# First norm of a two-layer decoder trunk: its factors moved into weight splits and copies, x loaded in halves, TensorE busy from the start

## The chip, the cores and the metric

The kernel runs on one core of one Trainium2 chip. The metric is the device time of one execution in microseconds (us). Three runs of the kernel before gave 1243.56 to 1244.70 us, with a median of 1244.01 us.

## What is computed

The program is a decoder trunk of two layers for 512 tokens of 1024 channels in float32. Only its opening matters here: the first norm and the input projection of the first layer.

```python
def rms_norm(x, g):
    y = x * lax.rsqrt(jnp.mean(x * x, axis=-1, keepdims=True) + NORM_EPS)
    return y * g

h = rms_norm(x, mix_norm_g[0])                     # (512, 1024)
a_q, a_k, a_v, b_q, b_k, b_v = split(h @ ab_w_in)  # 3072 columns
a_q, a_k = apply_rope(a_q), apply_rope(a_k)        # then differential attention, 4 heads
```

Each row of `h` has one factor of its own (the inverse root of its mean square), and each channel has one gain.

## The kernel before

Tokens lie in four tiles of 128 (`t` 0 to 3). A matmul works on single-precision values in three passes: weights and activations are each split into a high part (`w_hi`, `hT_hi`) and what is left of them (`w_lo`, `hT_lo`), and the products hi·hi, hi·lo and lo·hi are added up in one bank of the matmul's accumulator memory `ps`. ScalarE makes the high parts, VectorE or GpSimd the low ones.

The opening runs as follows. For each token tile ScalarE squares `x` and adds up (`square`), VectorE and ScalarE make the inverse root (`tile_variance`, `root`, `rsqrt`), VectorE multiplies `x` by root and gain in one instruction over 1024 channels (`scale_x`, to `xn`). TensorE turns the tile in eight 128x128 pieces (`turn_xn`); ScalarE copies them out in two instructions of 512 columns (`turn_tile`, high part), VectorE takes the low part (`tile_lows`). TensorE then multiplies by the first 384 columns of the projection (`group_0(t, half)`: 12 matmuls of 384 columns for each half of the channels). These 384 columns are what one group of two heads needs. The weights come in tiles of 1536 columns (`w_raw`, two slots), one for each half of the channels.

After group 0 two pieces of the next group's projection are made (`part_product(1, u, ...)`). They need the weights' third tile, split by ScalarE (`split_hi(0, 2)`) and VectorE (`split_lo(2, 0)`). Rotary positions of group 0 are applied on GpSimd for tiles 0 and 1 and on VectorE for tiles 2 and 3 (`rope(2)`, `rope(3)`); TensorE turns the results (`turn_qk`, 12 transposes), ScalarE and VectorE split them (`head_highs`, `head_lows`), and attention begins with `scores("A", 0, 0)` (line L1577), followed by the next part of the projection (L1525) in a loop over four groups.

The order on each engine is written by hand; engines wait for each other by semaphores. Loads are issued by SyncE in the order of its code. The kernel is a list of such hand-made stages; what follows the opening is attention, an MLP, the second layer and a last norm.

## Time and profile before

| | |
|---|---|
| median of three runs | 1244.01 us |
| the profiled execution's own time | 1244.71 us |
| its span (first to last instruction) | 1242.9 us |
| TensorE busy | 1215.6 us, 98% |
| VectorE, ScalarE, GpSimd busy | 512.1, 483.5, 567.8 us |

The span is what the trace covers; 1.8 us of the execution lie around it. Times below are counted from the start of the span. A busy TensorE is one with a matmul in flight, at either clock.

### The profile page before, as it was taken

Reading aid. Unit: us, or ns where it says so; the run is one execution under the profiler, and the core shown is the slowest. Engines: PE = TensorE matmul, PEld = TensorE weight load, DVE = VectorE, ACT = ScalarE, POOL = GpSimd, SP = SyncE. Lnnn points to the kernel's source line nnn. Section 1 sums busy time; section 2 is a strip of 40 time slices with the busy share of each in tenths; the row PEclk is TensorE's granted clock in tenths of the full one; section 3 lists DMA queues with packets and bytes.
Section 4 is the critical chain, followed back from the end, with each engine's and each line's share of the span. In section 5 each row is a group of like instructions: output and inputs, shape, how many; then the busy total and the mean of one; then the engine's idle time right before and its main releaser. Section 6 shows DMA issues by size and latency. Waiting matters only on the chain.

```text
span 1242.9 us, 16982 instructions
## 1 busy us (share of the span) xinstructions
PE 1215.6 (98%) x6252; PEld 1042.5 (84%) x6256; DVE 512.1 (41%) x907; ACT 483.5 (39%) x698; POOL 567.8 (46%) x501
## 2 busy tenths in 40 slices
PE   6999999999999999999999999999999999999997
PEld 6999999888888888888889879878888888888886
DVE  6777767745121211332342265634412221232325
ACT  4454544435232222433333365443523232333334
POOL 1444455334444444566655331611444444456662
PEclk9999999999999999999999999999999999999999
DMA  7212211212222222222213210300322222222221
GB/s 265 102 67 71 99 69 68 69 68 85 102 101 101 101 94 91 85 102 101 102 68 119 102 69 35 136 35 34 119 101 73 98 100 101 101 85 91 95 102 68
DMA packets 17037, 114.23 MB, mean 92 GB/s; under 512 B 1888, under 2 KB 2016, under 8 KB 4320
## 3 DMA queue, kind: packets, MB, share of 16 engines
q1 hardware_dynamic: 16416, 111.51, 24.8%
q10 hardware_dynamic: 576, 2.10, 0.6%
q8 instruction: 31, 0.51, 0.2%
q14 instruction: 14, 0.11, 0.0%
HBM read 111.50 MB, written 2.10 MB: 91 GB/s over the span
## 4 chain that ended last, share of the span: by engine, by line
PE 88%; POOL 4%; DVE 3%; ACT 1%; issue 1%; DMA 1%; POOLq 0%; SPq 0%; DVEq 0%; ACTq 0%
PE ps L1448 38%; PE ps L1738 16%; PE ps L1525 6%; PE ps L1391 6%; PE ps L1493 4%; PE ps L1420 3%; PE ps L1851 2%; PE ps L1438 2%; PE ps L1566 2%; PE ps L1831 2%; POOL tmp L327 1%; PE ps L1774 1%; POOL qk L333 1%; PE ps L1552 1%; PE ps L1348 1%
## 5 line engine op out<-in xcount | busy, mean ns | idle before, releaser
L303 POOL TENSOR_TENSOR w_lo<-w_raw,w_hi 128x512 fp32r<-128x512 f32 (+1 forms) x326 | 457.7, 1434 | 530.2 <-ACT w_hi L382 471.3
L382 ACT ACTIVATE w_hi<-w_raw 128x2048 fp32r<-128x2048 f32 (+1 forms) x95 | 175.3, 1845 | 309.6 <-PE ps L1448 155.2
L1448 PE MATMUL ps<-hT_hi,w_hi 128*128 128x512 f32 x688 | 267.7, 389 | 0.0
L1448 PE MATMUL ps<-hT_hi,w_lo 128*128 128x512 f32 x688 | 267.7, 389 | 0.0
L1448 PE MATMUL ps<-hT_lo,w_hi 128*128 128x512 f32 x688 | 267.6, 389 | 0.0
L1448 PEld LDWEIGHTS ps<-hT_lo,w_hi 128*128 128x128 f32 x688 | 129.1, 188 | 27.0
L1448 PEld LDWEIGHTS ps<-hT_hi,w_lo 128*128 128x128 f32 x688 | 129.1, 188 | 26.7
L1448 PEld LDWEIGHTS ps<-hT_hi,w_hi 128*128 128x128 f32 x688 | 129.1, 188 | 26.6
L1115 DVE TENSOR_TENSOR hT_lo<-region,hT_hi 128x2048 fp32r<-128x2048 f32 (+1 forms) x22 | 58.9, 2686 | 144.0 <-ACT hT_hi L640 144.0
L1085 DVE SCALAR_TENSOR_TENSOR qk<-ps,vec,qk 128x511 f32<-128x511 f32 x44 | 33.0, 750 | 200.1 <-ACT qk L614 200.1
L614 ACT ACTIVATE qk<-ps,vec 128x512 f32<-128x512 f32 x44 | 34.3, 780 | 175.5 <-PE ps L1448 166.3
L1738 PE MATMUL ps<-w_hi,hT_hi 128*128 128x512 f32 x256 | 99.6, 389 | 0.0
L1738 PE MATMUL ps<-w_lo,hT_hi 128*128 128x512 f32 x256 | 99.6, 389 | 0.0
L1738 PE MATMUL ps<-w_hi,hT_lo 128*128 128x512 f32 x256 | 99.6, 389 | 0.0
L1095 DVE TENSOR_TENSOR region<-ps,qk 128x512 f32 (+1 forms) x44 | 30.4, 691 | 155.4 <-PE ps L1448 155.4
L327 POOL TENSOR_TENSOR tmp<-region,cst 128x256 f32<-128x256 f32 x30 | 30.3, 1010 | 123.1 <-DVE region L926 98.4
L1525 PE MATMUL ps<-w_hi,hT_hi 128*128 128x384 f32 x224 | 80.5, 360 | 0.2 <-ACT region L498 0.2
L1525 PE MATMUL ps<-w_hi,hT_lo 128*128 128x384 f32 x224 | 75.2, 336 | 0.0
L1525 PE MATMUL ps<-w_lo,hT_hi 128*128 128x384 f32 x224 | 74.1, 336 | 0.0
L1738 PEld LDWEIGHTS ps<-w_lo,hT_hi 128*128 128x128 f32 x256 | 48.0, 188 | 10.0
L1738 PEld LDWEIGHTS ps<-w_hi,hT_hi 128*128 128x128 f32 x256 | 48.0, 188 | 10.0
L1738 PEld LDWEIGHTS ps<-w_hi,hT_lo 128*128 128x128 f32 x256 | 48.0, 188 | 9.9
(235 smaller groups left out, 2102.0 us busy)
## 6 DMA issues: line engine op xcount, KB each, us to landing
w_raw<-weights SPq DMA_DIRECT2D x99, 1024.0 KB, 4.8
x<-x_in SPq DMA_DIRECT2D x4, 512.0 KB, 8.8
gain<-gains ACTq DMA_DIRECT2D x4, 512.0 KB, 3.5
out<-region SPq DMA_DIRECT2D x4, 512.0 KB, 2.6
w_raw<-weights SPq DMA_DIRECT2D x2, 768.0 KB, 8.0
cst<-consts SPq DMA_DIRECT2D x1, 640.0 KB, 11.9
gain<-gains SPq DMA_DIRECT2D x1, 512.0 KB, 4.2
region<-masks SPq DMA_DIRECT2D x1, 384.0 KB, 12.2
```

The source lines that it names most:

```text
L303: ins = pool.tensor_tensor(w_lo[:, slot, cols], w_raw[:, slot, cols], w_hi[:, slot, cols].bitcast(f32), ALU.subtract)
L327: own.mark(pool.tensor_tensor(t1, src, cos, ALU.mult))
L382: sc.activation(w_hi[:, slot, 0:used], w_raw[:, slot, 0:used], ACT.Copy).then_inc(w_hi_ready, 1)
L614: sc.activation(qk[:, s, :], ps[:, s, :], ACT.Identity, scale=vec[:, ds(8 * i + (col + 2), 1)], bias=vec[:, ds(8 * i + (col + 3), 1)]).the ...
L1085: own.link(ve.scalar_tensor_tensor(qk[:, s, 1:SEQ], ps[:, s, 0:SEQ - 1], vec[:, ds(8 * i + (col + 1), 1)], qk[:, s, 1:SEQ], ALU.mult, ALU. ...
L1115: ve.tensor_tensor(hT_lo[:, places, :], act[:, ds(kt, count), :], hT_hi[:, places, :].bitcast(f32), ALU.subtract).then_inc(act_lo[l], count)
L1391: ins = pe.matmul(ps[:, bank, :], h[:, k0 + k, t * 128:(t + 1) * 128], w[:, slot, k * 512:(k + 1) * 512], start=first and (k, m) == produc ...
L1420: ins = pe.matmul(ps[:, s, 256 * half:256 * half + 256], w[:, slot, k * 256 + 128 * s:k * 256 + 128 * s + 128], h[:, k, 256 * half:256 * h ...
L1448: ins = pe.matmul(bank, w[:, slot, k * pitch + 128 * s:k * pitch + 128 * s + 128], h[:, k:k + 1, :], start=k == 0 and n == 0, stop=k == KT ...
L1493: ins = pe.matmul(ps[:, bank or 4 + f % 2, :], h_[:, place + k, t * 128:(t + 1) * 128], w_[:, (n0 + c) % 2, k * 512:(k + 1) * 512], start= ...
L1525: ins = pe.matmul(ps[:, bank, 0:384], h_[:, 4 * half + k, t * 128:(t + 1) * 128], w_[:, half, k * 384:(k + 1) * 384], start=first and k == ...
L1738: ins = pe.matmul(ps[:, 4 * c + t, :], a[:, t * 128:(t + 1) * 128], w[:, slot, u * 512:(u + 1) * 512], start=first and u == units[0] and n ...
```

## The change

- `x` is turned as it is, without root or gain. The gain of a channel is one number for each partition once the channels lie on partitions, and is put in where the high and low parts are made: `gained_high` on ScalarE and `gained_low` on VectorE, each four instructions of 128 columns with the gain as a per-partition operand, in place of one or two of 512 columns without one. The gains lie in `cst`, and the 512 KB load of the first gain row is gone.
- The inverse root of each token goes into the copies out of `ps` for all eight groups of the first projection (`copy_whole`, `add_part`, `copy_low`), as a per-partition operand `rstd_in`. One chain computes it for all four tiles.
- `x` is loaded in halves of 512 channels, tile 0's first half on ScalarE's queue; the identity and the first half of the first weight tile are issued first.
- TensorE multiplies eight times with a tile of ones that nothing reads (`warm`).
- All four tiles go through the first half of the channels, then all four through the second. VectorE now makes the third weight tile's low part ahead of both `rope` calls, and TensorE makes all passes of the two parts ahead of `turn_qk`.
- `copy_low(1, 0, 4)` stands ahead of `head_highs(0)`; `ident_bf`, `mask_bf` and `sub_gain` are made behind the ropes.

```diff
+        def load_x(eng, t0, t1, c, loaded):
+            src = x_in[0, t0 * 128:t1 * 128, c:c + 512].rearrange("(t p) n -> p t n", p=128)
+            eng.dma_start(x[:, t0:t1, c:c + 512], src).then_inc(loaded, 16)
...
-        FIRST_BANK = (6, 2, 4, 6)
+        FIRST_BANK = (6, 7, 2, 3)
+        FIRST_TURN = (0, 1, 4, 5)
...
-            load_x(sp, 0)
-            sp.dma_start(gain[:, :], gains[:, 0, :]).then_inc(gain_loaded, 16)
             sp.dma_start(cst[:, 0:C_CMUL], consts[:, 0:C_CMUL]).then_inc(ident_loaded, 16)
-            load(0, 0, IN_COLS)
-            load_x(sp, 1)
+            sp.dma_start(w_raw[:, 0, 0:768], weights[0, :, 0:768]).then_inc(first_loaded, 16)
+            sp.dma_start(w_raw[:, 0, 768:IN_COLS], weights[0, :, 768:IN_COLS]).then_inc(w_loaded[0], 16)
+            load_x(sp, 1, 2, 0, front_loaded[1])
+            load_x(sp, 2, 4, 0, front_loaded[2])
             load(1, 1, IN_COLS)
-            for t in range(2, NT):
-                load_x(sp, t)
+            load_x(sp, 0, 4, 512, back_loaded)
             sp.dma_start(cst[:, C_CMUL:], consts[:, C_CMUL:]).then_inc(cst_loaded, 16)
...
                 sc.wait_ge(mm_done, 8 * g + (u + 1))
-                sc.activation(y[:, u, ds(384 * g, 384)], ps[:, bank, 0:384], ACT.Copy).then_inc(part_low, 1)
+                sc.activation(y[:, u, ds(384 * g, 384)], ps[:, bank, 0:384], ACT.Copy, scale=rstd_in[:, u:u + 1])\
+                  .then_inc(part_low, 1)
...
+            load_x(sc, 0, 1, 0, front_loaded[0])
             sc.preload_act_table_set("sqrt_and_others")
-            square(0, 0)
-            root(0, 1)
+            def gained_high(half, t):
+                sc.wait_ge(turned, 4 * half + t + 1)
+                for j in range(4):
+                    k = 4 * half + j
+                    ins = sc.activation(hT_hi[:, k, t * 128:(t + 1) * 128], ps[:, FIRST_TURN[t], 128 * j:128 * j + 128],
+                                        ACT.Copy, scale=cst[:, C_GAIN + k:C_GAIN + k + 1])
+                ins.then_inc(turn_hi, 1)
+            def square_in(t):
+                scratch = stage_mem[:, :] if t else tmp[:, :, :].rearrange("p a n -> p (a n)")
+                sc.activation(scratch, x[:, t, :], ACT.Square, accum_out=ss[:, t:t + 1]).then_inc(ss_ready, 1)
...
+            gained_high(0, 0)
             sc.wait_ge(w_loaded[0], 16)
-            sc.activation(w_hi[:, 0, 0:768], w_raw[:, 0, 0:768], ACT.Copy).then_inc(w_hi_ready, 1)
-            turn_tile(0)
-            square(0, 1)
+            sc.activation(w_hi[:, 0, 768:IN_COLS], w_raw[:, 0, 768:IN_COLS], ACT.Copy).then_inc(w_hi_ready, 1)
+            gained_high(0, 1)
+            gained_high(0, 2)
             split_hi(1, 1, IN_COLS)
-            root(1, 2)
...
+            gained_high(0, 3)
+            sc.wait_ge(front_loaded[0], 16)
+            sc.wait_ge(back_loaded, 16)
+            square_in(0)
+            gained_high(1, 0)
+            sc.wait_ge(front_loaded[1], 16)
+            square_in(1)
+            gained_high(1, 1)
+            gained_high(1, 2)
+            root(0, 4)
+            gained_high(1, 3)
             turns[0] += 1
...
-            for n in range(2):
...
+            sc.wait_ge(mm_done, 1)
+            split_hi(0, 2, IN_COLS)
             sc.wait_ge(lam_dots, 1)
             sc.activation(lam_s[:, 2:4], lam_s[:, 0:2], ACT.Exp).then_inc(lam_exps, 1)
+            sc.wait_ge(mm_done, 8)
+            split_hi(1, 2, IN_COLS)
+            sc.wait_ge(scale_ready, 1)
+            copy_low(1, 0, 4)
+            head_highs(0)
...
                 ve.wait_ge(mm_done, (2, 4, 6, 8)[t])
-                ve.tensor_copy(y[:, t, 0:384], ps[:, FIRST_BANK[t], 0:384]).then_inc(part_sum, 1)
+                ve.tensor_scalar(y[:, t, 0:384], ps[:, FIRST_BANK[t], 0:384], rstd_in[:, t:t + 1], None, ALU.mult)\
+                  .then_inc(part_sum, 1)
...
                 ve.wait_ge(part_low, 4 * (g - 1) + (u - 3))
                 dst = y[:, u - 4, ds(384 * g, 384)]
-                ve.tensor_tensor(dst, dst, ps[:, 4 + u % 2, 0:384], ALU.add).then_inc(part_sum, 1)
+                ve.scalar_tensor_tensor(dst, ps[:, 4 + u % 2, 0:384], rstd_in[:, u - 4:u - 3], dst, ALU.mult, ALU.add)\
...
+            def gained_low(half, t):
+                ve.wait_ge(turn_hi, 4 * half + t + 1)
+                for j in range(4):
+                    k = 4 * half + j
+                    hi = hT_hi[:, k, t * 128:(t + 1) * 128]
+                    ins = ve.scalar_tensor_tensor(hT_lo[:, k, t * 128:(t + 1) * 128],
+                                                  ps[:, FIRST_TURN[t], 128 * j:128 * j + 128],
+                                                  cst[:, C_GAIN + k:C_GAIN + k + 1], hi.bitcast(f32),
+                                                  ALU.mult, ALU.subtract)
+                ins.then_inc(turn_lo, 1)
...
+            def first_part_low(cols, made):
+                ve.tensor_tensor(w_lo[:, 0, cols], w_raw[:, 0, cols], w_hi[:, 0, cols].bitcast(f32),
+                                 ALU.subtract).then_inc(made, 1)
+            ve.wait_ge(first_loaded, 16)
+            ve.tensor_copy(w_hi[:, 0, 0:768], w_raw[:, 0, 0:768]).then_inc(first_high, 1)
             ve.wait_ge(first_high, 1)
-            split_lo(0, 0, IN_COLS)
-            tile_lows(0)
...
-            rsqrt(1, 2)
-            scale_x(0, 1, xn)
+            first_part_low(slice(0, 768), first_low)
+            ve.wait_ge(ident_loaded, 16)
+            gained_low(0, 0)
+            ve.wait_ge(w_hi_ready, 1)
+            first_part_low(slice(768, IN_COLS), w_lo_ready)
+            gained_low(0, 1)
+            gained_low(0, 2)
             split_lo(1, 1, IN_COLS)
-            tile_variance(0, 2)
...
+            gained_low(0, 3)
+            square_in(2)
+            gained_low(1, 0)
+            gained_low(1, 1)
+            square_in(3)
+            ve.wait_ge(ss_ready, 4)
+            variance(0, 4, 1.0 / DM)
+            gained_low(1, 2)
+            rsqrt(0, 4, rstd_in)
+            ve.sem_inc(scale_ready, 1)
             copy_whole(0)
-            rsqrt(3, 4)
...
+            gained_low(1, 3)
             turns[0] += 1
             copy_whole(1)
-            ve.wait_ge(ident_loaded, 16)
-            own.mark(ve.tensor_copy(ident_bf[:, :], ident))
-            ve.wait_ge(cst_loaded, 16)
...
               .then_inc(lam_dots, 1)
-            own.mark(ve.tensor_scalar(sub_gain[:, :], vec[:, V_SUB:V_SUB + 128], 1.0 - LAM_INIT, None, ALU.mult))
+            split_lo(2, 0, IN_COLS)
+            ve.wait_ge(cst_loaded, 16)
...
-            split_lo(2, 0, IN_COLS)
-            head_lows(0)
+            own.mark(ve.tensor_copy(ident_bf[:, :], ident))
+            ve.wait_ge(mask_loaded, 16)
+            ve.tensor_copy(mask_bf[:, :], masks_f32).then_inc(masks_ready, 1)
+            own.mark(ve.tensor_scalar(sub_gain[:, :], vec[:, V_SUB:V_SUB + 128], 1.0 - LAM_INIT, None, ALU.mult))
             ve.wait_ge(lam_exps, 1)
             own.link(ve.tensor_tensor(neg_lam[:, :], lam_s[:, 3:4], lam_s[:, 2:3], ALU.subtract))
             own.link(ve.tensor_scalar(neg_lam[:, :], neg_lam[:, :], -LAM_INIT, None, ALU.add))
+            head_lows(0)
...
+            def turn_in(half, t):
+                if half == 0:
+                    pe.wait_ge(front_loaded[min(t, 2)], 16)
+                else:
+                    pe.wait_ge(back_loaded, 16)
+                    pe.wait_ge(turn_lo, t + 1)
+                for j in range(4):
+                    c = 512 * half + 128 * j
+                    ins = pe.transpose(ps[:, FIRST_TURN[t], 128 * j:128 * j + 128], x[:, t, c:c + 128], ident)
+                ins.then_inc(turned, 1)
+            def group_0(t, half, passes=(0, 1, 2), units=range(4), inc=0):
+                for n in passes:
+                    pe.wait_ge(turn_lo if n == 2 else turn_hi, 4 * half + t + 1)
                     h_, w_ = PASSES[n]
-                    for k in range(4):
-                        if t == 0 and half == 0 and n == 0 and k == 2:
-                            pe.wait_ge(first_high, 1)
+                    for k in units:
                         ins = pe.matmul(ps[:, FIRST_BANK[t], 0:384], h_[:, 4 * half + k, t * 128:(t + 1) * 128],
-                                        w_[:, half, k * 384:(k + 1) * 384],
-                                        start=half == 0 and n == 0 and k == 0,
-                                        stop=half == 1 and n == 1 and k == 3)
+                                        w_[:, half, k * 384:(k + 1) * 384], start=half == 0 and n == 0 and k == 0,
+                                        stop=half == 1 and n == 2 and k == 3)
                 if inc:
                     ins.then_inc(mm_done, inc)
-            turn_xn(0)
...
+            def warm(count):
+                for _ in range(count):
+                    pe.matmul(ps[:, 7, :], mask_bf[:, 0:128], mask_bf[:, 0:512], start=True, stop=True)
+            pe.wait_ge(warm_ready, 1)
+            warm(6)
+            pe.wait_ge(ident_loaded, 16)
+            turn_in(0, 0)
+            warm(2)
+            pe.wait_ge(first_high, 1)
+            group_0(0, 0, (0,), (0, 1))
+            pe.wait_ge(first_low, 1)
+            group_0(0, 0, (1,), (0, 1))
+            pe.wait_ge(w_hi_ready, 1)
+            group_0(0, 0, (0,), (2, 3))
+            turn_in(0, 1)
+            group_0(0, 0, (2,))
+            pe.wait_ge(w_lo_ready, 1)
+            group_0(0, 0, (1,), (2, 3))
+            for t in range(1, NT):
+                group_0(t, 0, (0, 1))
+                if t < 3:
+                    turn_in(0, t + 1)
+                else:
+                    turn_in(1, 0)
+                group_0(t, 0, (2,), inc=int(t == 3))
+            pe.wait_ge(w_hi_ready, 2)
+            pe.wait_ge(w_lo_ready, 2)
+            for t in range(NT):
+                group_0(t, 1, (0, 1))
+                if t < 3:
+                    turn_in(1, t + 1)
+                group_0(t, 1, (2,), inc=(1, 2, 2, 2)[t])
             turns[0] += 1
             norms[0] += 1
             pe.wait_ge(w_hi_ready, 3)
-            for u, bank in ((0, 3), (1, 5)):
+            for u, bank in ((0, 4), (1, 5)):
                 part_product(1, u, bank, (0, 2), True, False)
+            pe.wait_ge(w_lo_ready, 3)
+            for u, bank in ((0, 4), (1, 5)):
+                part_product(1, u, bank, (1,), False, True)
             turn_qk(0, at_once=True)
-            pe.wait_ge(w_lo_ready, 3)
-            for u, bank in ((0, 3), (1, 5)):
-                part_product(1, u, bank, (1,), False, True)
```

On TensorE at the program's start, before (`cst,xn` is a transpose of normalised x, the others are `group_0`):

```order
L1348 MATMUL ps<-cst,xn 128x128 x8
L1774 MATMUL ps<-w_hi,hT_hi 128x384 x4
L1774 MATMUL ps<-w_lo,hT_hi 128x384 x4
L1774 MATMUL ps<-w_hi,hT_lo 128x384 x4
L1348 MATMUL ps<-cst,xn 128x128 x8
L1774 MATMUL ps<-w_hi,hT_hi 128x384 x4
```

and in the change (`mask_bf` is the tile of ones, `cst,x` a transpose of x):

```order
L1834 MATMUL ps<-mask_bf 128x512 x6
L1817 MATMUL ps<-cst,x 128x128 x4
L1834 MATMUL ps<-mask_bf 128x512 x2
L1826 MATMUL ps<-w_hi,hT_hi 128x384 x2
L1826 MATMUL ps<-w_lo,hT_hi 128x384 x2
L1826 MATMUL ps<-w_hi,hT_hi 128x384 x2
L1817 MATMUL ps<-cst,x 128x128 x4
L1826 MATMUL ps<-w_hi,hT_lo 128x384 x4
L1826 MATMUL ps<-w_lo,hT_hi 128x384 x2
L1826 MATMUL ps<-w_hi,hT_hi 128x384 x4
L1826 MATMUL ps<-w_lo,hT_hi 128x384 x4
L1817 MATMUL ps<-cst,x 128x128 x4
```

Ten matmuls now stand around the first four transposes, and transposes come in fours between the passes of a tile.

On ScalarE, from the second token tile to the third weight tile's split, before (L442 copies out the high parts, L679 loads the table for exp, L382 splits weights):

```order
L442 ACTIVATE hT_hi<-ps 128x4x128 x2
L415 ACTIVATE sd<-var 128x1
L432 ACTIVATE tmp,ss<-x 128x1024
L415 ACTIVATE sd<-var 128x1
L442 ACTIVATE hT_hi<-ps 128x4x128 x4
L679 ACT_TABLE_LOAD
L406 DMA gain<-gains 128x1024
L382 ACTIVATE w_hi<-w_raw 128x1536 x2
```

and in the change, from the second half's first tile (L671 is `gained_high`, L678 the square, L418 the root, L699 the table, L385 the split):

{{act_a}}

Each pair of 512-column copies has become eight of 128 columns; the table load and the split still follow the last of them.

On VectorE around the ropes, before (L919 `copy_whole`, L1181 to L1186 `rope`, L843 the third weight tile's low part, L910 and L913 `head_lows`):

```order
L919 COPY region<-ps 128x384
L1181 TENSOR_TENSOR xn<-region,cst 128x256
L1182 TENSOR_TENSOR xn<-region,cst 128x4x32
L1183 TENSOR_TENSOR xn<-region,cst 128x4x32
L1184 TENSOR_TENSOR qk<-xn 128x128
L1186 TENSOR_TENSOR qk<-xn 128x256
L843 TENSOR_TENSOR w_lo<-w_raw,w_hi 128x1536
L910 SCALAR_TENSOR_TENSOR q_split<-ps,q_split 64x512
L913 TENSOR_TENSOR k_low<-ps,k_high 128x512
```

and in the change (L1167 `gained_low`, L941 `copy_whole`, L1212 and L1213 the lambda products, L865 the weights' low part, L1225 to L1230 `rope`):

```order
L1167 SCALAR_TENSOR_TENSOR hT_lo<-ps,cst,hT_hi 128x128 x4
L941 TENSOR_SCALAR region<-ps,rstd_in 128x384
L1212 TENSOR_TENSOR o_tmp<-vec 128x64 x2
L1213 TENSOR_REDUCE lam_s<-o_tmp 128x2
L865 TENSOR_TENSOR w_lo<-w_raw,w_hi 128x1536
L941 TENSOR_SCALAR region<-ps,rstd_in 128x384
L1225 TENSOR_TENSOR xn<-region,cst 128x256
L1226 TENSOR_TENSOR xn<-region,cst 128x4x32
L1227 TENSOR_TENSOR xn<-region,cst 128x4x32
L1228 TENSOR_TENSOR qk<-xn 128x128
L1230 TENSOR_TENSOR qk<-xn 128x256
```

The low part of the weights has moved from behind the second rope to ahead of the first.

## Rows read from the trace of the kernel before

**Rows 1.** The page, part 1.

```profile
PE 1215.6 (98%) x6252; PEld 1042.5 (84%) x6256; DVE 512.1 (41%) x907; ACT 483.5 (39%) x698; POOL 567.8 (46%) x501
```

**Rows 2.** Waits, 0 to 90 us: who waited for whom, total us, times, longest.

```profile
PE ps L1348 <- DVE xn L869: 9.9, 2, 7.9
...
PE ps L1577 <- DVE k_low L913: 0.4, 1, 0.4
```

**Rows 3.** Timeline, TensorE, 7 to 17 us: start, us, engine, line, operation.

```profile
7.89 1.94 PE L1348 MATMUL ps<-cst,xn 128*128 128x128 f32 x8 [7.89 <-DVE xn L869]
10.38 1.62 PE L1774 MATMUL ps<-w_hi,hT_hi 128*128 128x384 f32 x4 [0.55 <-ACT hT_hi L442]
11.79 1.52 PE L1774 MATMUL ps<-w_lo,hT_hi 128*128 128x384 f32 x4
```

**Rows 4.** Windows around the clock change; PEclk is the granted clock.

```profile
core 0: us, PE busy (x) PEld busy (x) DVE busy (x) ACT busy (x) POOL busy (x), PEclk, DMA share, GB/s
14.05:16.03 1.98, 0.00 (x0) 0.00 (x0) 1.84 (x6) 0.87 (x2) 0.00 (x0) 1.00 1.01 408
...
16.64:20.05 3.41, 3.41 (x14) 3.41 (x13) 3.27 (x9) 2.32 (x5) 0.00 (x0) 0.50 1.02 387
```

**Rows 5.** Timeline, TensorE, 20 to 24 us.

```profile
22.02 0.86 PE L1774 MATMUL ps<-w_lo,hT_hi 128*128 128x384 f32 x4
22.71 1.03 PE L1348 MATMUL ps<-cst,xn 128*128 128x128 f32 x8
```

**Rows 6.** Timeline, ScalarE, 7 to 47 us.

```profile
8.91 0.84 ACT L666 ACTIVATE w_hi<-w_raw 128x768 fp32r<-128x768 f32 x1 [3.26 <-DMA w_raw<-weights]
...
23.35 1.09 ACT L442 ACTIVATE hT_hi<-ps 128x512 fp32r<-128x512 f32 x2 [2.17 <-PE ps L1348]
...
27.42 1.28 ACT L679 ACT_TABLE_LOAD   x1
...
35.10 1.49 ACT L382 ACTIVATE w_hi<-w_raw 128x1536 fp32r<-128x1536 f32 x1 [2.67 <-PE ps L1774]
38.96 0.59 ACT L491 ACTIVATE q_split<-ps 64x512 fp32r<-64x512 f32 x1 [2.38 <-PE ps L1515]
...
43.05 0.37 ACT L518 ACTIVATE xn<-ps,neg_max 128x128 f32<-128x128 f32 x1 [0.92 <-DVE neg_max L951]
43.31 0.19 ACT L518 ACTIVATION_READ_ACCUMULATOR xn<-ps,neg_max 128x1 f32 x1
```

**Rows 7.** ScalarE groups by form: busy us, mean ns.

```profile
L442 ACT ACTIVATE hT_hi<-ps 128x512 fp32r<-128x512 f32 x32 | 17.3, 587 | 7.0 <-PE ps L1348 7.0
...
L726 ACT ACTIVATE hT_hi<-ps,vec 128x512 fp32r<-128x512 f32 x5 | 3.2, 687 | 0.8 <-PE ps L1864 0.8
...
L527 ACT ACTIVATE xn<-ps 128x128 f32<-128x128 f32 x4 | 1.1, 263 | 0.0
```

**Rows 8.** DMA issues, first 1 us: KB, us to landing.

```profile
x<-x_in SPq DMA_DIRECT2D x1, 512.0 KB, 3.3
```

**Rows 9.** Timeline, VectorE and GpSimd, 28.5 to 38 us.

```profile
28.77 1.12 POOL L327 TENSOR_TENSOR tmp<-region,cst 128x256 f32<-128x256 f32 x1 [3.55 <-DVE region L919]
...
29.21 1.18 DVE L1169 TENSOR_TENSOR o_tmp<-vec 128x64 f32<-128x64 f32 x2
...
33.02 0.56 DVE L919 COPY region<-ps 128x384 f32<-128x384 f32 x1 [2.17 <-PE ps L1774]
...
34.02 0.28 DVE L1182 TENSOR_TENSOR xn<-region,cst 128x128 f32<-128x128 f32 x1
...
36.83 0.42 DVE L1186 TENSOR_TENSOR qk<-xn 128x256 f32<-128x256 f32 x1
...
37.16 1.75 DVE L843 TENSOR_TENSOR w_lo<-w_raw,w_hi 128x1536 fp32r<-128x1536 f32 x1
```

**Rows 10.** Timeline, TensorE, 37.6 to 42 us.

```profile
37.67 1.47 PE L1515 MATMUL ps<-cst,qk 128*128 128x128 f32 x12
...
41.05 0.33 PE L1577 MATMUL ps<-k_high,q_split 128*128 128x128 f32 x1 [0.42 <-DVE k_low L913]
...
41.71 0.44 PE L1525 MATMUL ps<-w_hi,hT_hi 128*128 128x384 f32 x1 [0.15 <-ACT region L498]
```

103 lines of the change are left out of this document (30 added, 73 removed).

## The prediction

> **What bounds the kernel now.** I read the page first: TensorE is busy for 1215.6 of 1242.9 us [rows 1]. So an edit is worth what it takes from, or adds to, the time at which TensorE can run on without waiting. The waits of the first 90 us say where that is. TensorE lost 9.9 us in two waits for VectorE's normalised x (`scale_x`), 7.9 of them before its first matmul, and 0.4 us for `head_lows` [rows 2]. The first instructions ran slowly: eight transposes in 1.94 us, and four matmuls of 384 columns in 11.79 - 10.38 = 1.41 us [rows 3], where later four take 0.69 us and eight transposes follow a pass at 22.71 and are over in 1.03 us [rows 5]. After the second wait, 14.05 to 16.03, the granted clock fell to half (1.2 GHz instead of 2.4) from 16.64 to 20.05 [rows 4]. So the opening is badly used, and several us are to be had in it. But how much reaches the end is settled at one place: attention's first matmul, L1577, starts at 41.05 [rows 10]. From there TensorE is fed without a break worth naming, by code that the change hardly touches. I take the difference at L1577 as the difference of the whole.
>
> **What the change takes away.** The chain square, root, scale no longer stands before the first transpose. Its share, VectorE's and ScalarE's work, was the 7.9 and 2.0 us of waits. In its place TensorE waits for x's half tile alone. A whole tile (512 KB) landed 3.3 us after its issue [rows 8], at 4.0 us. Half of it could land at 3.4, but the identity and weights share the DMA engines; I take 4.0 (bounds 3.4 to 4.6). The eight warm matmuls are not in the trace. Matmuls of 384 columns took 0.35 us each at the slow clock [rows 3], so I estimate 0.45 for 512 columns, six in 2.7 us. Started at about 1.2 us they end at 3.9, before the data; the last two lie beside ScalarE's first copies. They cost nothing; if x came at 3.4, they would cost 0.5 us.
>
> **How long a half tile now takes.** This is the term on which the sum rests. In the new order a pass pair of tile t is followed by the transposes of tile t+1, the third pass of t, and then a wait for `gained_high` of t+1. TensorE's own work is 8 matmuls (1.39 us at 0.69 for four), four transposes (0.4) and 4 matmuls (0.69): 2.5 us. The way over ScalarE is 1.39 us, then 0.64 from the first transpose to the copy's start (22.71 to 23.35 [rows 5, 6]), then the copies, then 0.1 for the signal. Before, 512 columns were one copy of 0.587 us [rows 7], two in 1.09 [rows 6]. Now they are four of 128 columns with a per-partition gain. A per-partition operand adds 0.1 us at 512 columns (687 against 587 ns), and a plain copy of 128 columns takes 263 ns [rows 7]. The nearest row is the 128-column exp with such an operand: 0.37 us, the next instruction 0.26 us behind its start (43.05, 43.31 [rows 6]). Four make 3 x 0.265 + 0.37 = 1.16 us. The lower bound is a plain copy's 0.263 with 0.17 between starts (the same 0.1 overlap): 0.78. The upper is 0.37 each without overlap: 1.5. I take 1.16, since operand, width and engine are those of the row. The way over ScalarE is then 1.39 + 0.64 + 1.16 + 0.1 = 3.3 us, which is 0.8 more than TensorE's own work. TensorE waits 0.8 us in each half tile (bounds 0.4 and 1.15). The two squares on ScalarE (1.25 us each) and VectorE's low parts (four short instructions against 1.8 us of room) fit beside it; the last of x, 3.7 MB into the queue at some 390 GB/s [rows 4], lands at about 12.5 us and is needed at 17.
>
> The Trainium skill speaks against this edit. ScalarE: Activation LUTs, section "What ACT_TABLE_LOAD costs", says that a [128,1] operand adds about 93 ns to each ACTIVATE, and that back-to-back ones overlap by as much. Its formula gives 387 ns and 294 between starts, 1.27 us for four. The trace agrees on the addition (100 ns) and shows a shorter step (265). By the page the sum below would be 0.9 us larger (eight runs of copies, 0.11 each).
>
> **The start.** x at 4.0; four transposes at the slow rate, 1.0; to ScalarE 0.2; copies 1.16: 6.4. The second part of the first weight tile, 0.84 on ScalarE [rows 6]: 7.25. TensorE makes two matmuls on it (0.5 with the signal): 7.85. Transposes of tile 1 and signal 0.64, copies 1.16, signal 0.1: tile 1 starts at 9.75. Six half tiles at 3.3 bring the last one's start to 29.55, and ScalarE's last copy had ended 0.1 before, at 29.45. (In the trace of before, that last copy ended at 27.4, where the table load starts [rows 6].)
>
> **The handover.** From that moment a chain runs that before lay in the shadow of matmuls. Table load 1.28, high part of weight tile 3 1.49 [rows 6], signals 0.1, its low part 1.75 on VectorE [rows 9]: 34.1. Only then do the two ropes start, which have been put behind it: 33.02 to 37.25, 4.23 us [rows 9]. I add 0.1 for the per-partition factor in two copies and 0.2 because GpSimd ropes tile 1 meanwhile (beside it two 64-column products took 1.18 us, where one of 128 columns later took 0.28 [rows 9]): 38.6. Signal 0.1, transposes to the first head copy 1.29 (37.67 to 38.96), heads 2.09 (38.96 to 41.05) [rows 6, 10]: L1577 at 42.1. TensorE has meanwhile finished group 0 (31.7) and the 24 matmuls of the two parts (4.2 us, from 32.4 to 36.6): it waits 0.7, then 2.0 for the ropes, runs 1.4 us of transposes, and waits 2.1 for the heads. Before, eight matmuls filled the last gap (L1577 waited 0.42 [rows 10]).
>
> **The sum.** 42.1 - 41.05 = +1.05. The copy that held L1525 for 0.15 us [rows 10] is made earlier: -0.15. Factors in 28 copies and sums of the attention loop are off the path but for the last of a group: +0.1 to +0.4, I take +0.2. The clock: in the trace one wait of 2.0 us was followed by 3.41 us at half clock [rows 4], which cost 1.7 us of work. Now two such waits lie 1.4 us apart. I expect one fall, partly inside the second wait: +1.2 (bounds 0 and 2.6). Together +2.3 us. The profiled execution took 1244.71 us, 0.7 above the median; the difference goes onto the median, 1244.0 + 2.3 = 1246.3 us. A measurement of this kernel tells some 0.2% (2.5 us) from no change, so this is slower, but at the edge.
>
> **The rivals.**
> Cheap copies (0.78 us for four): each half tile 2.9 us. Eight such runs of copies save 0.38 each: 3.0. L1577 at 39.1, and with the fall of the clock 1243.3. For it: the source is the matmul's memory and two copies overlap well. Against: rows 7.
> The clock holds: 1246.3 - 1.2 = 1245.1. For it: each wait is at most as long as the one before the fall. Against: there are two now.
> Slower: half clock through two stretches. If the fall comes in the gap at 38 us, the head wait keeps TensorE idle, and it starts attention slowly; the stretch is then paid whole and part of a second: +2.6 in place of +1.2, and 0.4 for the copies of the loop: 1247.9. This decides as soon as more than 1.4 us is lost to the clock.
> Faster: TensorE does not wait for ScalarE in the half tiles at all. This needs the way over ScalarE to be 2.5 us, so copies of under 0.4 us. Six waits of 0.8 and 0.8 in each of the two runs of the start go, 6.4 us: L1577 at 35.7 and the time 1239.9. From copies of 0.55 us down the kernel is faster by more than 0.2% (eight times 0.6 is 4.8 us off 1246.3). For it: the 9.9 us of waits at the start are real, and overlapping copies may be shorter than the exp. Against: even one copy of 512 columns took 0.59 [rows 7].
>
> **Chances.** The forecast 0.45, at the bound of what can be told: 0.23 slower, 0.22 same. Cheap copies 0.14, same. Clock holds 0.13, same. Two stretches 0.13, slower. Faster 0.15. So faster 0.15, same 0.49, slower 0.36. The range: the bounds of the copies give -3.0 and +1.5 or so (half of the upper one is unlikely), those of x and the clock -1.2 and +1.4; 1242.0 to 1248.8 leaves out most of the faster case and the far end of the slower.
>
> **What would show it.** Right: the first transpose at about 4 us; `gained_high` four instructions some 0.27 us apart; TensorE idle 0.8 us before each half tile, waiting for `hT_hi`; the last `gained_high` ends near 29.5; a wait of 2 us before `turn_qk` with VectorE's rope as its cause; L1577 near 42; a stretch at half clock between 37 and 46. Wrong: L1577 before 39, or no wait for the ropes; or a clock that falls in the half tiles too, since TensorE idles a quarter of them.

## The result, and the profile after

The changed kernel takes 1251.11 us (median of 6 runs, 1247.76 to 1252.06) against 1244.07 us before (6 runs on the same chip, 1243.56 to 1245.16). The ratio is 1.0048, 95% interval 1.0038 to 1.0058. It is slower, by 7 us where 2.3 were forecast, and the forecast range ended at 1248.8. The profiled execution took 1251.75 us, its span 1249.9 us (before: 1242.9). The six runs lie apart with TensorE's mean granted clock: 1247.76 us at 0.998, four at 0.995 or 0.996, 1252.06 at 0.993.

Part 1 of the page, to be read beside [rows 1]:

```profile
PE 1221.8 (98%) x6260; PEld 1043.5 (83%) x6264; DVE 512.8 (41%) x918; ACT 488.2 (39%) x715; POOL 568.7 (46%) x501
```

TensorE is busy 6.2 us longer, with eight matmuls more. These eight are 3.7 us of it (2.74 and 0.93 us, the `warm` calls). The rest is not more work but slower work: a matmul at half clock, and a first one after a wait, have longer rows. The waits of TensorE in the first 60 us (total, times, longest), against the 9.9 + 0.4 us of [rows 2]:

```profile
PE ps L1826 <- ACT hT_hi L671: 3.9, 7, 0.7
...
PE ps L1563 <- DVE qk L1230: 2.5, 1, 2.5
...
PE ps L1625 <- DVE k_low L935: 1.8, 1, 1.8
...
PE ps L1826 <- ACT w_hi L683: 1.2, 1, 1.2
```

The two waits for `scale_x`, 7.9 and 2.0 us, are gone, and ten others of 0.5 to 2.5 us have come: seven for the half tiles' high parts, one for the second half of the first weight tile, one for the ropes, one for the heads. TensorE's timeline shows where they stand (start, busy us, and in brackets the idle time before it with its cause):

```profile
4.39 1.09 PE L1817 MATMUL ps<-cst,x 128*128 128x128 f32 x4 [0.18 <-DMA x<-x_in]
...
9.47 1.01 PE L1826 MATMUL ps<-w_hi,hT_hi 128*128 128x384 f32 x2 [1.18 <-ACT w_hi L683]
10.28 1.06 PE L1817 MATMUL ps<-cst,x 128*128 128x128 f32 x4
...
12.93 0.86 PE L1826 MATMUL ps<-w_hi,hT_hi 128*128 128x384 f32 x4
...
32.92 0.97 PE L1826 MATMUL ps<-w_hi,hT_hi 128*128 128x384 f32 x4 [0.52 <-ACT hT_hi L671]
...
42.69 2.11 PE L1563 MATMUL ps<-cst,qk 128*128 128x128 f32 x12 [2.52 <-DVE qk L1230]
46.57 0.48 PE L1625 MATMUL ps<-k_high,q_split 128*128 128x128 f32 x1 [1.77 <-DVE k_low L935]
```

The last row answers to L1577 in [rows 10]: attention's first matmul starts at 46.57 instead of 41.05, 5.5 us later. Tile 1 starts at 12.93 and the last half tile at 32.92, so a step between half tiles is 19.99 / 6 = 3.33 us.

The chain that ended last, in order of time (start, us, what), says why tile 1 is late, and what the end of the stage consists of:

```profile
1.67 6.88 DMA w_raw<-weights
...
8.58 0.85 ACT w_hi L683
...
9.47 1.01 PE ps L1826 x2
...
32.90 1.13 DVE hT_lo L1167 x4
...
34.56 0.62 DVE o_tmp L1212
...
35.20 0.66 DVE o_tmp L1212
...
35.92 0.17 issue
36.08 1.75 DVE w_lo L865
```

Behind its issue by SyncE the chain is one transfer up to 8.55 us, the second 384 KB of the first weight tile. And VectorE reaches the low part of weight tile 3 at 36.08, behind its own lambda products, although ScalarE had the high part ready at 35.67. ScalarE's rows from its last copy on:

```profile
31.72 0.37 ACT L671 ACTIVATE hT_hi<-ps,cst 128x128 fp32r<-128x128 f32 x1 [2.10 <-PE ps L1817]
...
31.99 0.88 ACT L671 ACTIVATE hT_hi<-ps,cst 128x128 fp32r<-128x128 f32 x3
32.88 1.28 ACT L699 ACT_TABLE_LOAD   x1
34.18 1.49 ACT L385 ACTIVATE w_hi<-w_raw 128x1536 fp32r<-128x1536 f32 x1
```

The clock, in windows cut at its changes (the columns are those of [rows 4]):

```profile
9.36:12.77 3.41, 3.30 (x12) 3.21 (x13) 1.18 (x2) 1.20 (x5) 0.00 (x0) 0.50 1.02 405
43.49:50.32 6.83, 5.06 (x20) 4.66 (x19) 4.76 (x7) 3.19 (x7) 0.00 (x0) 0.50 0.00 1
```

This column reads 1.00 before the first rise in both kernels, though the matmuls there are slow, so that part is read from TensorE's rows. Those of the change are slow up to about 6 us, those of before up to about 13: behind the two slow passes of [rows 3] comes the first fast one,

```profile
13.11 0.94 PE L1774 MATMUL ps<-w_hi,hT_lo 128*128 128x384 f32 x4
```

After this first rise the change is at half clock (1.2 GHz) for 10.2 us, where before it was for 3.4 [rows 4]: once behind the wait for the weights, and for twice as long from 43.49, behind the wait for the ropes, over the transposes, the wait for the heads and 3.75 us of attention.

### The profile page after: what moved, and what is told of

It reads as the page before. It is cut to its first block, busy times and chain, and to the rows that moved or that the text cites. A ratio compares the mean times of both kernels' runs of the same rounds, so it can differ in the third digit from the quotient of the medians.

```text
span 1249.9 us, 17031 instructions
## 1 busy us (share of the span) xinstructions
PE 1221.8 (98%) x6260; PEld 1043.5 (83%) x6264; DVE 512.8 (41%) x918; ACT 488.2 (39%) x715; POOL 568.7 (46%) x501
## 4 chain that ended last, share of the span: by engine, by line
PE 88%; POOL 4%; DVE 3%; ACT 2%; issue 1%; DMA 1%; POOLq 0%; SPq 0%; DVEq 0%; ACTq 0%
PE ps L1496 37%; PE ps L1786 16%; PE ps L1573 6%; PE ps L1439 6%; PE ps L1541 4%; PE ps L1468 3%; PE ps L1922 2%; PE ps L1614 2%; PE ps L1486 2%; PE ps L1902 2%; POOL tmp L330 1%; PE ps L1600 1%; PE ps L1826 1%; POOL qk L336 1%; PE ps L1963 1%
## 5 line engine op out<-in xcount | busy, mean ns | idle before, releaser
L385 ACT ACTIVATE w_hi<-w_raw 128x2048 fp32r<-128x2048 f32 (+1 forms) x95 | 175.3, 1846 | 304.2 <-PE ps L1496 155.2
## 6 DMA issues: line engine op xcount, KB each, us to landing
cst<-consts SPq DMA_DIRECT2D x1, 640.0 KB, 12.2
```

The costliest lines, as they stand in the source:

```text
L385: sc.activation(w_hi[:, slot, 0:used], w_raw[:, slot, 0:used], ACT.Copy).then_inc(w_hi_ready, 1)
```

## The experiments

Each edits the changed kernel. Differences in us are of medians: to the changed kernel's 1251.1, and to the kernel before, which took 1244.4 to 1244.6 beside them (1244.1 beside the change). The changed kernel's own six runs spread over 4.3 us, so a difference under 1 us between two of these kernels says little. The runs of a2, a3, b1, b3, b4 and c4, five each, overlap with those six, so their differences from it, up to 2.7 us, are uncertain by one to two microseconds; those of a1, a4, b2, c1 and c2 rest on eleven runs.

**a1_turn_first: the next half tile is turned ahead of all three passes.**

```diff
-                group_0(t, 1, (0, 1))
                 if t < 3:
                     turn_in(1, t + 1)
-                group_0(t, 1, (2,), inc=(1, 2, 2, 2)[t])
+                group_0(t, 1, inc=(1, 2, 2, 2)[t])
```

(and the same for half 0).

> The changed kernel with one edit: the transposes of the next half tile stand ahead of all twelve matmuls of a half tile, not between them. Main theory (the way over ScalarE, 1.4 us of matmuls, 0.65 to the copy and 1.14 of copies, is longer than TensorE's own 2.5 us and sets the step of 3.33 us from half tile to half tile): the waits of 0.8 us for hT_hi go, the step falls to about 2.5 us, the last half tile starts near 28 instead of 32.92, L1625 (the first scores) comes near 41.5 instead of 46.57, and the time falls by 4.5 to 5.5 us. Rival 1 (what was lost is lost at the start and at the handover; the waits for ScalarE are only shadows of late transfers of x or of VectorE's work): the step stays above 3.1 us and the time falls by less than 1.5 us.

Measured: 1246.18 us (11 runs, 1241.4 to 1248.48), ratio to before 1.0007 [0.9996, 1.0019]; 5 us less than the change. The transposes of successive half tiles, from TensorE's timeline:

```profile
16.01 0.60 PE L1817 MATMUL ps<-cst,x 128*128 128x128 f32 x4
...
18.55 0.60 PE L1817 MATMUL ps<-cst,x 128*128 128x128 f32 x4
```

The step is 2.54 us, TensorE's own work, with no wait in it. L1625 starts at 42.59, 4.0 us earlier. The step of 3.3 was indeed the way over ScalarE, and only the order made it so: the same copies, started a pair of passes earlier, are hidden. The rest of the 5 us goes with the clock: in this profile it was full again at 41.4, before attention began. The waits for the ropes and the heads stayed (2.75 and 1.77 us), as the theory had it.

**a4_whole_copies: one copy of 512 columns for each half tile, without the channels' gains, which the result then lacks.**

```diff
-                for j in range(4):
-                    k = 4 * half + j
-                    ins = sc.activation(hT_hi[:, k, ...], ps[:, FIRST_TURN[t], 128 * j:128 * j + 128],
-                                        ACT.Copy, scale=cst[:, C_GAIN + k:C_GAIN + k + 1])
-                ins.then_inc(turn_hi, 1)
+                sc.activation(hT_hi[:, 4 * half:4 * half + 4, ...], ps[:, FIRST_TURN[t], :], ACT.Copy).then_inc(turn_hi, 1)
```

(and one subtraction on VectorE in place of four).

> The changed kernel, but the high part of a half tile is made by one copy of 512 columns on ScalarE and the low part by one subtraction on VectorE. This leaves the channel gains of the first norm out of the result; nothing else is left out. Theory pieces (four copies with a per-partition operand, 1.14 us against 0.59, are what makes the way over ScalarE too long): each step from half tile to half tile falls from 3.33 to 2.75 us, eight copies save 0.55 each, L1625 comes near 42.5 and the time falls by 4 us. Rival (the place of the transposes, not the pieces, decides, and the copies' length is hidden): the step stays above 3.1 us, the time falls by less than 1.5 us.

Measured: 1248.02 us (11 runs), 1.0026 [1.0016, 1.0035]; 3.1 us less than the change. ScalarE by shape, in the change and here:

```profile
L671 ACT ACTIVATE hT_hi<-ps,cst 128x128 fp32r<-128x128 f32 x32 | 9.1, 368 | 15.0 <-PE ps L1817 15.0
```

```profile
L669 ACT ACTIVATE hT_hi<-ps 128x512 fp32r<-128x512 f32 x8 | 4.8, 598 | 15.6 <-PE ps L1810 15.6
```

Four small copies take 1.14 us (368 ns each, overlapping), one large one 0.60. The step falls by as much, from 3.33 to 2.80 (16.55 to 19.36 between two turns). So the gains in the copies cost 0.54 us in each half tile. It is less than a1's 0.8, because a pair of passes still stands ahead of the turn.

**a2_ropes_first: the ropes ahead of weight tile 3's low part, `turn_qk` ahead of the parts' low pass.**

```diff
-            split_lo(2, 0, IN_COLS)
             ve.wait_ge(cst_loaded, 16)
...
             rope(3)
+            split_lo(2, 0, IN_COLS)
...
+            turn_qk(0, at_once=True)
             pe.wait_ge(w_lo_ready, 3)
             for u, bank in ((0, 4), (1, 5)):
                 part_product(1, u, bank, (1,), False, True)
-            turn_qk(0, at_once=True)
```

> The changed kernel with the handover's order taken back: VectorE makes both ropes ahead of the third weight tile's low part, and TensorE turns q and k between the two groups of passes, as before the change. Main theory (the handover chain with the low part ahead of the ropes is what delays L1625, and its two waits pull the clock down): the ropes end near 40.5 instead of 42.6, L1625 comes near 44 instead of 46.57, the gaps of 2.5 and 1.8 us shrink to one of about 2, and the time falls by 2.6 us if the clock still falls, by 4.5 us if it holds. Rival (the ropes are bound by GpSimd's work beside them or by the last copies, not by the low part): L1625 moves by less than 1 us and the time by less than 1.5 us.

Measured: 1250.8 us (5 runs), 1.0051 [1.0038, 1.0065]; 0.3 us less. `turn_qk` starts 2.4 us earlier, at 40.31, but L1625 at 46.35. ScalarE's row tells where the gain went:

```profile
43.73 0.58 ACT L498 ACTIVATE region<-ps,rstd_in 128x384 f32<-128x384 f32 x1 [6.78 <-PE ps L1573]
44.21 0.58 ACT L491 ACTIVATE q_split<-ps 64x512 fp32r<-64x512 f32 x1
```

In the changed kernel `copy_low` stands ahead of `head_highs` on ScalarE. It waits for the part's last pass, which now comes behind the transposes, and the heads wait behind it. That pass, eight matmuls, also took 2.93 us at half clock, where it takes 1.66 at full (b1). I had looked at VectorE and TensorE only; neither theory had this.

**b1_handover_back: the whole handover in the order of before.** As a2, and:

```diff
             sc.wait_ge(mm_done, 8)
             split_hi(1, 2, IN_COLS)
+            head_highs(0)
             sc.wait_ge(scale_ready, 1)
             copy_low(1, 0, 4)
-            head_highs(0)
```

with VectorE's casts and lambda products ahead of the ropes, and the lambda exp behind `copy_low`.

> The changed kernel with the whole handover put back: VectorE casts the identity and the masks ahead of the lambda products, makes the ropes, then the third weight tile's low part, then the heads; ScalarE does the heads ahead of copy_low; TensorE turns q and k between the two groups of passes. The opening up to the end of group 0 stays as changed. In the run with only the ropes moved, turn_qk came 2.4 us earlier but L1625 did not, because ScalarE's copy_low stood ahead of the heads and waited for the part's last pass. Main theory (the handover as changed costs about 2 us beside the clock): L1625 near 44.4 instead of 46.57; the time falls by 2 us, by up to 4 if the clock holds. Rival (the late end of group 0 carries it all and the handover's order is free): L1625 above 46, the time falls by less than 0.7 us.

Measured: 1248.39 us (5 runs), 1.0038 [1.0024, 1.0051]; 2.7 us less. The gap before L1625 is gone, as 8 matmuls stand in it again, but TensorE waits 2.95 us for the ropes:

```profile
40.22 1.53 PE L1563 MATMUL ps<-cst,qk 128*128 128x128 f32 x12 [2.95 <-DVE qk L1233]
41.89 1.66 PE L1573 MATMUL ps<-w_lo,hT_hi 128*128 128x384 f32 x8
```

The order of before does not make the ropes early when the last half tile comes late; it fills one of the two gaps. What that is worth without the clock can be read from two profiles: from the last half tile's first matmul to L1625 it is 12.2 us here (31.41 to 43.65) and 13.3 in c4 (31.46 to 44.76), which has the changed order; neither profile has a stretch at half clock there. So the order itself gives 1.1 us. Most of the rest of L1625's lead over the change (46.57) lies in the start, where tile 1 came 1.6 us earlier (11.32) by the same instructions.

**b2_turn_and_handover: a1, and the handover led past the last half tile.** ScalarE makes weight tile 3's high part before the last copies:

```diff
             root(0, 4)
+            sc.wait_ge(mm_done, 1)
+            split_hi(0, 2, IN_COLS)
             gained_high(1, 3)
```

VectorE makes the lambda products and casts between low parts, then the ropes, then weight tile 3's low part; the rest as b1.

> The changed kernel with the transposes ahead of all passes of a half tile (as in the first run of this series), the third weight tile's high part made ahead of the last copies and of the table load, the lambda products and the casts of identity and masks made between the low parts, the ropes directly behind the last low part, the weights' low part behind them, ScalarE's heads ahead of copy_low, and q and k turned between the passes. Main theory (with the wait for ScalarE's copies and the serial handover gone, what is left is TensorE's own work after a start that is 1 us better than before the change): last copy near 28, turn_qk near 34, L1625 near 37.5, no long wait and no half clock there; the time is 1240.5 to 1241.5, 3 us below the kernel before. Rival (something else holds L1625, or the loop over the groups has become slower by the factors in its copies and gives it back): 1243 or more.

Measured: 1242.21 us (11 runs), 0.9982 [0.9973, 0.9991]: 8.9 us less than the change and 2.2 less than before. The table load now stands behind the split (ScalarE's timeline):

```profile
24.27 1.47 ACT L385 ACTIVATE w_hi<-w_raw 128x1536 fp32r<-128x1536 f32 x1
...
25.64 1.12 ACT L671 ACTIVATE hT_hi<-ps,cst 128x128 fp32r<-128x128 f32 x4
26.78 1.28 ACT L701 ACT_TABLE_LOAD   x1
```

and L1625 starts at 39.13. The two edits alone gave 5.0 and 2.7, and this kernel 8.9. It holds more than their sum, the weight split ahead of the last copies and VectorE's work moved forward; what each of these gives was not measured by itself. TensorE still waits 2.27 us for the ropes.

**b3_whole_weights: the first weight tile in one transfer.**

```diff
-            sp.dma_start(w_raw[:, 0, 0:768], weights[0, :, 0:768]).then_inc(first_loaded, 16)
-            sp.dma_start(w_raw[:, 0, 768:IN_COLS], weights[0, :, 768:IN_COLS]).then_inc(w_loaded[0], 16)
+            sp.dma_start(w_raw[:, 0, 0:IN_COLS], weights[0, :, 0:IN_COLS]).then_inc(w_loaded[0], 16)
```

> The changed kernel, but the first weight tile comes in one transfer of 768 KB, as before the change, instead of two halves of 384 KB. The trace of the change shows the halves' packets of 3072 bytes at 189 ns each, against 281 ns for 6144 bytes before. Theory packets (the halving makes the weights late: 8.58 us for the second half): the whole tile lands near 7.7, the second transposes start 0.6 to 1 us earlier than 10.28, and the time falls by 0.7 us or so. Rival 1 (the bytes ahead in the queues set the landing): it lands at 8.3 or later and the time is the same or, as the first matmuls start later, longer. Rival 2: the halves come back through the clock, the time moves by over 1.5 us.

Measured: 1249.7 us (5 runs), 1.0044 [1.003, 1.0057]; 1.4 us less. Its chain of waits, where the change's stood at 1.67 + 6.88:

```profile
1.20 5.04 DMA w_raw<-weights
6.24 0.02 issue
6.26 0.57 DVE w_hi L1184
```

All 768 KB are there at 6.24. In the change the first half came at 6.07, the second at 8.55. Splitting the transfer brought the first half 0.2 us forward and the second 2.3 us back. The other profiles say the same: in the nine with two halves the second was there between 7.9 and 8.9 us, in the three with one transfer (b3, c2, c3) all of it between 6.2 and 6.4. Tile 1's first matmul moves from 12.93 to 10.51, and L1625 from 46.57 to 44.94: 0.7 of the gain goes to transposes that now lie wholly at half clock.

**b4_no_warm: without the eight warm matmuls.**

```diff
-            warm(6)
...
-            warm(2)
```

> The changed kernel without the eight matmuls on the tile of ones. Theory cover (they cost nothing, since data come later than they end, and gain little, since the clock falls again in the wait for weights from 8.3 to 9.5): the time moves by less than 1 us. Rival gain (they do save a stretch at half clock): the time rises by 1 to 1.7 us. Rival cost (they bring about the fall at 8.9 us, because the clock had risen early and then saw a wait): without them the clock rises at about 9 and stays, the time falls by 1 us.

Measured: 1251.63 us (5 runs), 1.0052 [1.0038, 1.0066]; 0.5 us more, which is within the spread. The clock is slow up to 13.41 here, as two of TensorE's rows show (two matmuls of 384 columns in 1.01 us, then four in 0.87):

```profile
9.83 1.01 PE L1826 MATMUL ps<-w_hi,hT_hi 128*128 128x384 f32 x2 [1.35 <-ACT w_hi L683]
...
13.41 0.87 PE L1826 MATMUL ps<-w_hi,hT_hi 128*128 128x384 f32 x4
```

In the change it is full from about 6, but falls again at 9.36. But these two profiles do not show what the warm matmuls did: a1 has all eight of them, and its rows are slow up to about 14 us (a2's up to about 11):

```profile
12.94 1.05 PE L1817 MATMUL ps<-cst,x 128*128 128x128 f32 x4
...
14.60 0.88 PE L1826 MATMUL ps<-w_lo,hT_hi 128*128 128x384 f32 x4
```

So only the medians can tell, and they show no gain that is clear of the spread.

**a3_fill_gaps: nine unread matmuls before `turn_qk`, seven behind it.**

```diff
+            pe.wait_ge(part_sum, 2)
+            fill(9)
             turn_qk(0, at_once=True)
+            fill(7)
```

> The changed kernel with nine matmuls that nothing reads (512 columns, bank 7) ahead of the transposes of q and k and seven behind them, in the two waits of 2.5 and 1.8 us. They are short enough to end inside the waits. Theory clock (the stretch at half clock from 43.0 to 49.9 follows from the two waits and costs some 2.1 us: 0.4 in the transposes and 1.65 behind 46.57): the clock holds in this stretch, L1625 comes at 46.2, the time falls by 2 us. Rival (the clock falls for another reason, or the matmuls delay the heads): the half clock stays or the time does not fall by more than 0.7 us.

Measured: 1250.03 us (5 runs), 1.004 [1.0026, 1.0054]; 1.1 us less. The late stretch is gone, but the one at the start is twice as long in the profiled execution:

```profile
7.63:14.45 6.82, 6.03 (x20) 5.43 (x21) 2.92 (x9) 1.99 (x5) 0.00 (x0) 0.50 1.03 405
14.45:60.00 45.55, 41.02 (x238) 36.84 (x236) 32.18 (x77) 23.51 (x54) 11.64 (x16) 1.00 0.33 120
```

The edit leaves the first 14 us of instructions as they were, and yet the clock fell at 7.63 for 6.8 us where in the change it fell at 9.36 for 3.4. So when and for how long it falls there is not set by the instructions alone, one profile can't price the clock, and this run gives no clean number for it.

**c4_fill_all_gaps: unread matmuls in every long wait, the one for the first weights too.** As a3, and `warm(4)` behind the first transposes, `warm(5)` ahead of the wait for `w_hi`.

> The changed kernel with matmuls that nothing reads in all its long gaps: two more behind the first transposes, five ahead of the wait for the second half of the first weights, nine ahead of turning q and k and seven behind. Theory clock (the two stretches at half clock cost 1.3 and 2.1 us): no half clock after the first rise, tile 1's matmuls start at 12 instead of 12.93, L1625 near 45.3, the time is 1247.5 to 1248.5, 3 us below the change and still 3.5 above the kernel before. Rival (the fillings cost what they save): 1250 or more.

Measured: 1248.39 us (5 runs, 1247.99 to 1250.18), 1.0036 [1.0022, 1.005]; 2.7 us less. No stretch at half clock is left after 4.55:

```profile
4.55:60.00 55.45, 49.91 (x283) 43.20 (x283) 38.73 (x92) 27.69 (x66) 13.63 (x20) 1.00 0.46 168
```

So the clock costs the change some 2.7 us, and 3.9 us over the kernel before are left that no fall of the clock explains. The change's own fastest run, 1247.76 us at a mean clock of 0.998, is 3.7 over it.

**c1_turn_handover_fill: b2 with nine unread matmuls before `turn_qk`.**

> The kernel b2 (transposes first, handover rearranged) with nine matmuls that nothing reads (512 columns) in its last gap, the 2.3 us ahead of turning q and k. Theory clock (the wait brings about the half clock from 35.8 to 39.3, which costs some 1.7 us: slow transposes and eight slow matmuls): the clock holds there, L1625 comes at 38 instead of 39.1, the time falls by 1 to 1.7 us to 1240.5 to 1241.2. Rival (the heads' chain on ScalarE and VectorE bounds L1625 at either clock): less than 0.5 us.

Measured: 1242.7 us (11 runs), 0.9985 [0.9976, 0.9994]; 0.5 us more than b2, no gain. In its profile too the late stretch is gone and the one at the start runs from 8.38 to 15.21, where b2's ran from 8.53 to 11.94. Holding the clock in one late place alone gave nothing that could be measured (a3: 1.1 us, within the spread).

**c2_turn_handover_weights: b2 with the first weight tile in one transfer.**

> The kernel b2 with the first weight tile in one transfer, as in b3, where the second transposes came at 8.68 instead of 10.28. Theory packets: the same 1 to 1.6 us are won here, and the time falls by 1 us to 1241.2 or less. Rival (x and the second weight tile land too late for an earlier start, or the clock takes it back): less than 0.4 us.

Measured: 1240.68 us (11 runs), 0.9972 [0.9963, 0.9981]; 1.5 us less than b2, as the same edit gave on the change alone (1.4).

**c3_all: c2, nine unread matmuls before `turn_qk`, four warm ones behind the first transposes.**

> The kernel b2 with the filling matmuls of c1, the whole weight tile of c2, and four instead of two warm matmuls behind the first transposes. If the savings of c1 and c2 add up (main theory): 1239 to 1240, about 0.4% below the kernel before. Rival (they overlap, since the clock's stretch moves with the start): as the better of the two.

Measured: 1239.96 us (6 runs), 0.9968 [0.9956, 0.998]: the fastest, 11 us less than the change and 4.5 less than before. TensorE's rows at the end of the stage:

```profile
30.43 2.25 PE L1837 MATMUL ps<-w_hi,hT_hi 128*128 128x512 f32 x9
32.89 1.53 PE L1562 MATMUL ps<-cst,qk 128*128 128x128 f32 x12 [0.21 <-DVE qk L1232]
34.55 1.68 PE L1572 MATMUL ps<-w_lo,hT_hi 128*128 128x384 f32 x8
```

The clock does not fall once. `turn_qk` starts no earlier than in c2 (32.67), since the fill only stands where TensorE waited; c3's gain over c2, 0.7 us, is no larger than the spread.

## Why the prediction was wrong

The direction was right, though the prediction gave it only 0.36 and no change to be told 0.49, and so were the chain and most of its terms. The size was not: 7.0 us instead of 2.3. The difference of 4.7 us is made up of four parts. In the profiled execution they come to 3.2 (start), 0.2 (six steps of 3.33 instead of 3.3), 1.0 (handover) and 0.2 (behind L1625, where 7.0 - 5.5 = 1.5 us were lost and 1.25 forecast), 4.6 together.

**The start failed: "The second part of the first weight tile, 0.84 on ScalarE [rows 6]: 7.25.", and from it "tile 1 starts at 9.75".** (The sum has a slip of 0.1 in it: 7.25 and 0.5 are 7.75.) I let that split begin as soon as ScalarE had made its copies, at 6.4, and asked only what the engine would take. Nothing there asked when its data would be there. It landed at 8.55, and ScalarE waited 1.85 us for it. The row that says so was among those I had quoted: in the kernel before, the same split began at 8.91 after 3.26 us of waiting for that tile [rows 6]. The change puts its transfers earlier in the queue, but as two halves, and b3 shows that this alone costs 2.3 us of landing (measured time: 1.4 us). The other 1.0 us of the start is the clock: from the split's end to tile 1 I forecast 2.5 us, and at half clock it took 3.5 (9.42 to 12.93). With the same instructions at full clock b1 took 2.35 (8.97 to 11.32).

**The clock was mis-sized: "I expect one fall, partly inside the second wait: +1.2 (bounds 0 and 2.6)".** The rival "half clock through two stretches" is what the late part did: 6.8 us from 43.49. Of these L1625 lost 0.4 (the transposes' 1.72 us instead of 1.29) and attention an estimated 1.7 (3.75 us in which a matmul of 384 columns took 0.32 us, where 0.17 is usual). But I had looked for a fall only in the handover. There was a second one at the start, beside a wait of 1.2 us that I had not forecast. c4 prices both together at about 2.7 us against my 1.2, at my upper bound of 2.6. The term varies from run to run, as the change's six runs show. Before, the clock had fallen once as well, behind a wait of 2.0 us [rows 4], and its matmuls had been slow up to about 13 us; the time of before contains both.

**The handover was 1.0 us short: 13.7 us from ScalarE's last copy to L1625, where the forecast had 12.65.** The table load and the high part were right to 0.02 us. Then 0.3 is VectorE's: I had the low part start when the high part was there, but VectorE's order, shown ahead of the prediction, has the lambda products before it, and beside GpSimd's rope they took 1.38 + 0.28 us and ended behind it. Another 0.3 is the ropes, which took 4.8 us from the low part's end instead of the 4.5 forecast. The first one ran beside GpSimd's; its first two products and those of the second, from VectorE's timeline:

```profile
34.47 1.38 DVE L1212 TENSOR_TENSOR o_tmp<-vec 128x64 f32<-128x64 f32 x2
...
38.40 0.57 DVE L1225 TENSOR_TENSOR xn<-region,cst 128x256 f32<-128x256 f32 x1
38.90 0.82 DVE L1226 TENSOR_TENSOR xn<-region,cst 128x128 f32<-128x128 f32 x1
...
41.15 0.43 DVE L1225 TENSOR_TENSOR xn<-region,cst 128x256 f32<-128x256 f32 x1
41.49 0.28 DVE L1226 TENSOR_TENSOR xn<-region,cst 128x128 f32<-128x128 f32 x1
```

The last 0.4 is the transposes at half clock.

**Right were** the first transposes (4.39; 4.0 forecast), the copies (1.14 us for four; 1.16 forecast), the step (3.33; 3.3 forecast) and its cause, the wait for the ropes (2.52; 2.0) and for the heads (1.77; 2.1), and that the factors in attention's copies cost next to nothing (in c4 L1625 came 3.7 us late and the span was 3.5 longer). The idle time before each half tile reads 0.53, not 0.8, because the rows beside it take the rest: the last four matmuls' row is 0.16 longer than the 0.69 at which the next ones could start, and the first four after the wait take 0.80 instead of 0.69. The step, which takes that in, is the number to compare. The rival "TensorE does not wait for ScalarE" was ruled out by the change's own rows, in which each of the six steps has its wait for `hT_hi`.

The Trainium skill, ScalarE: Activation LUTs, section "What ACT_TABLE_LOAD costs", gave an estimate of 1.27 us for the four copies, with 294 ns between starts. The trace does not agree: 1.14 us for four and 368 ns for one, so 257 ns between starts. By the page's figure the forecast would have been 0.9 us larger, nearer the result for a wrong reason.

**What the change loses, then.** It removes 9.9 us of waits at the start and gives all of it back, and 7 us more. The edits that take them out again are: the turn behind two passes 5.0 us (a1), the handover 4.0 on top of a1 (b2), the split transfer 1.5 on top of both (c2). c2, which has all three, is 10.4 us under the change. Alone, in a1, b1 and b3, they gave 5.0, 2.7 and 1.4, 9.1 together, and part of each is the clock. The idea itself, no norm ahead of the first transpose, with its end reordered and its data in time, is then 3.8 us faster than the kernel before (c2), or 4.5 in the one with the clock held (c3), a difference within the spread.

**What stays open.** Why two transfers of 384 KB land so much later than one of 768 KB. The two kernels' DMA engines move about as much meanwhile (292 GB/s from 2 to 8.5 us in the change, 303 from 2 to 6.2 in b3), so the second half may have shared them with what was issued behind it. The trace's single packets fit that: of the two halves' 256 packets 41 start after 6.0 us, the last at 8.13, among some 300 packets of x's next loads, while in b3 all 128 of the tile have started by then. That keeping those loads back would bring the second half forward was not tried. And what decides when the clock first rises and how long it is at half at the start was not settled: a3 and c1 had 6.8 us, the change, a4 and b2 3.4, a1, a2 and b1 with the same opening none, but a1 and a2 rose late; c4 and c3, with more matmuls there, had none.

## What to carry to other kernels

Put the production of the next operand ahead of all the work that can hide it, not in its middle: the same copies cost 0.8 us a step behind two of three passes and nothing ahead of them. When a stage is rearranged, follow the last producer's engine past the stage's end, since what was in the shadow of the matmuls (here a table load, a weight split and two ropes) becomes the chain; move it ahead of the last copies where its inputs allow. And ask of every first use when its data lands, by the nearest row of the trace of before: an engine's readiness is not the data's.

## What the runs showed of the hardware that was not expected

- One transfer of 768 KB landed 5.0 us after its issue, complete. As two of 384 KB the first came after 4.9 us, the second after 6.9.
- The granted clock fell beside waits of 1.2 us (9.36, the one for the weights) and 2.5 us (43.49), but in no half tile, where TensorE idles 0.5 of every 3.3 us. A wait alone did not decide it: b1's profile has waits of 1.0 and 2.95 us and no fall. Kernels with the same first instructions had an early stretch of 3.4 us (the change, b2), of 6.8 (a3, c1) or none (a1, a2, b1) in their profiled executions, and their first rise lay between 4 and 14 us; filling only the late waits (a3, c1) moved the time by -1.1 and +0.5 us, and filling the early ones too by -2.7.
- Beside a rope on GpSimd, VectorE's two products of 64 columns took 1.38 us. Of GpSimd's own products of 128 columns one took 2.01 us, where its neighbours took 0.46:

```profile
35.72 0.46 POOL L331 TENSOR_TENSOR tmp<-region,cst 128x128 f32<-128x128 f32 x1
36.14 2.01 POOL L332 TENSOR_TENSOR tmp<-region,cst 128x128 f32<-128x128 f32 x1
38.23 0.46 POOL L334 TENSOR_TENSOR qk<-tmp 128x128 f32<-128x128 f32 x1
```

The 2.01 us begin with VectorE's low part of the weights (36.08 to 37.83) and end just behind it. No run moves the two apart, so that one delays the other is read from these times alone.
